# Spreading gate, scale and shift rows over the partitions: by DMA through a DRAM scratch instead of by TensorE

## The reference, cut to what matters

```python
    return rmsnorm(x, final_g)                      # end of the first part
...
    mods = jnp.split(c_silu @ ada_w[layer] + ada_b[layer], N_MOD, axis=-1)
    sh, sc, g = mods[0], mods[1], mods[2]
    h = modulate(rms_norm(x, norm_g[layer, 0]), sh, sc)      # h * (1 + sc) + sh
    x = x + MACARON_WEIGHT * (1.0 + g)[:, None, :] * swiglu(h, ffn_w_in[layer, 0], ffn_w_out[layer, 0])
    ...
    x = x + (1.0 + g)[:, None, :] * y               # y: pool mixer (layer 0) or causal attention (layer 1)
    ...
    x = x + MACARON_WEIGHT * (1.0 + g)[:, None, :] * swiglu(h, ffn_w_in[layer, 1], ffn_w_out[layer, 1])
```

## Time and profile before

| | |
|---|---|
| median of 3 runs | 1232.81 us (1232.74 to 1233.06) |
| the profiled execution | 1232.74 us, of which the span is 1230.9 |
| PE busy | 1199.6 us, 97% of the span |
| DVE, ACT, POOL busy | 66%, 48%, 47% |
| DMA | 293.18 MB, mean 238 GB/s |

### The profile page before, as it was taken

How to read it: one execution, slowest core, us unless ns; L and a number is a source line. 1 busy time by engine, 2 the same in 40 slices (tenths; PEclk the granted TensorE clock), 3 DMA queues, 4 the chain that set the end, 5 groups by cost and what they waited for, 6 DMA issues and landing times.

```text
span 1230.9 us, 15554 instructions
## 1 busy us (share of the span) xinstructions
PE 1199.6 (97%) x5816; PEld 985.0 (80%) x5816; DVE 807.3 (66%) x1116; ACT 592.3 (48%) x774; POOL 577.2 (47%) x424
## 2 busy tenths in 40 slices
PE   9999999999999999899999999999999999999998
PEld 6777887888788887788888878788888887888886
DVE  6885568855687778568778756597774675644433
ACT  5465564555643443454434356444342665534340
POOL 1365333655544534445453455754534463345360
PEclk9999999999999999999999999999999999999999
DMA  9976369744698898439889747699875444766650
GB/s 354 347 255 229 104 235 330 255 172 130 228 339 283 310 330 284 155 95 358 297 296 343 252 171 257 227 315 306 297 291 171 145 135 155 251 209 208 203 171 35
DMA packets 181657, 293.18 MB, mean 238 GB/s; under 512 B 8144, under 2 KB 99920, under 8 KB 181584
## 3 DMA queue, kind: packets, MB, share of 16 engines
q1 hardware_dynamic: 177552, 284.82, 67.7%
q10 hardware_dynamic: 4032, 7.38, 1.8%
HBM read 291.12 MB, written 1.05 MB: 237 GB/s over the span
## 4 chain that ended last, share of the span: by engine, by line
PE 86%; DVE 7%; ACT 3%; issue 2%; POOL 1%; DVEq 0%; ACTq 0%
PE ps L1767 50%; PE ps L1776 25%; PE ps L2027 2%; PE ps L1790 1%; PE ps L1855 1%; DVE w_lo L1129 1%; ACT w_hi L626 1%; PE ps L1912 1%; PE ps L1928 1%; PE ps L1940 1%; POOL w_lo L496 1%; DVE ps L1115 1%; DVE x L1223 1%; PE ps L1951 1%; POOL stat L487 1%
## 5 line engine op out<-in xcount | busy, mean ns | idle before, releaser
L496 POOL TENSOR_TENSOR w_lo<-raw,w_hi 128x512 fp32r<-128x512 f32 x356 | 497.7, 1430 | 448.5 <-ACT w_hi L626 448.5
L1767 PE MATMUL ps<-w_hi,h_hi 128*128 128x512 f32 x1120 | 444.6, 402 | 2.4 <-issue 1.4
L1767 PE MATMUL ps<-w_hi,h_lo 128*128 128x512 f32 x1120 | 432.8, 391 | 0.0
L626 ACT ACTIVATE w_hi<-raw 128x2048 fp32r<-128x2048 f32 x188 | 353.4, 1909 | 87.8 <-PE ps L1776 80.7
L1776 PE MATMUL ps<-w_lo,h_hi 128*128 128x512 f32 x1120 | 301.1, 391 | 5.3 <-DVE w_lo L1129 2.4
L1129 DVE TENSOR_TENSOR w_lo<-raw,w_hi 128x2048 fp32r<-128x2048 f32 x95 | 226.3, 2387 | 97.4 <-ACT w_hi L626 96.7
L1767 PEld LDWEIGHTS ps<-w_hi,h_hi 128*128 128x128 f32 x1120 | 210.3, 188 | 51.6 <-issue 11.2
L1776 PEld LDWEIGHTS ps<-w_lo,h_hi 128*128 128x128 f32 x1120 | 209.5, 188 | 52.4 <-DVE w_lo L1129 3.6
L1767 PEld LDWEIGHTS ps<-w_hi,h_lo 128*128 128x128 f32 x1120 | 211.2, 189 | 40.8
L1115 DVE SCALAR_TENSOR_TENSOR ps<-ada_raw,ccol,ps 128x512 f32<-128x512 f32 x240 | 181.1, 755 | 6.9 <-DMA ada_raw<-ada_w 0.2
L889 ACT ACTIVATE a_hi<-ps 128x512 fp32r<-128x512 f32 x44 | 26.3, 599 | 181.5 <-PE ps L2027 181.5
(11 more groups left out here) (195 smaller groups left out, 1002.6 us busy)
## 6 DMA issues: line engine op xcount, KB each, us to landing
raw<-ffn_in SPq DMA_DIRECT2D x176, 512.0 KB, 5.7
ada_raw<-ada_w SPq DMA_DIRECT2D x144, 512.0 KB, 7.2
raw<-ffn_out SPq DMA_DIRECT2D x44, 1024.0 KB, 5.5
raw<-w_in SPq DMA_DIRECT2D x31, 1024.0 KB, 8.4
raw<-w_out SPq DMA_DIRECT2D x8, 1024.0 KB, 5.9
ada_raw<-kv_ada_w SPq DMA_DIRECT2D x16, 512.0 KB, 7.5
raw<-w_kv SPq DMA_DIRECT2D x8, 1024.0 KB, 5.5
bias<-na_bias ACTq DMA_DIRECT2D x16, 256.0 KB, 3.7
```

The lines of the kernel that those rows point to most:

```text
L496: ins = pool.tensor_tensor(w_lo[:, u % RAW, piece], raw[:, u % RAW, piece], w_hi[:, u % RING, piece].bitcast(F32), ALU.subtract)
L626: act.activation(w_hi[:, u % RING, :], raw[:, u % RAW, :], ACT.Copy).then_inc(*S.inc("w_hi_ready", u))
L1767: pe.matmul(bank(b), part[:, k_in_lhs + k, tok], wh[:, k, c * 512:(c + 1) * 512], start=first_mm[c], stop=False)
```

## The change

The `make_row` function on PE and all its calls go, and `row_copy` on ACT. In their place ACT issues two DMAs per row: `row_store` writes the column block to one row of a scratch tensor `mod_rows` in DRAM, and `row_load`, after a wait for that store, reads this row once for each of the 128 partitions. The final norm's row is loaded from a new kernel input that holds `final_g` as one row. DVE waits for the load's semaphore.

```diff
+        ROWS = {("down", 0, 0): 2, "pool": 5, "pool_scale": 4, "pool_shift": 3, ("down", 0, 1): 8,
+                ("down", 1, 0): 13, "o": 16, ("down", 1, 1): 19}
+        mod_rows = nc.dram_tensor("mod_rows", (len(ROWS), D), F32, kind="Internal").ap()
+        row_of = {name: mod_rows[i:i + 1, :] for i, name in enumerate(ROWS)}
...
-            def row_copy(name, into=row):
-                for half in range(2):
-                    b = job_bank["row", name, half]
-                    act.wait_ge(*S.at("row_done", name, half))
-                    act.activation(into[:, half * 512:half * 512 + 512], bank(b), ACT.Copy).then_inc(
-                        *S.inc("row_ready", name, half))
+            def row_store(name):
+                act.wait_ge(*S.at("mod_ready", ROWS[name]))
+                act.dma_start(row_of[name].rearrange("o (k p) -> p (o k)", p=P), mods[:, ROWS[name], :], allow_slow_non_contiguous=True).then_inc(
+                    row_out[name], 16)
+            def row_load(name, into=row):
+                act.wait_ge(row_out[name], 16)
+                act.dma_start(into[:], row_of[name].broadcast_to([P, D])).then_inc(row_in[name], 16)
...
+                if layer == DEPTH - 1:
+                    act.dma_start(row[:], final_row.broadcast_to([P, D])).then_inc(row_in["final"], 16)
                 o = first["out", layer]
                 fill(o + 3)
...
             fill(first["up", 0, 0])
-            row_copy("final")
...
                 fill(d + 2)
                 high_act(NG - 1)
-                row_copy(("down", layer, i))
+                row_store(("down", layer, i))
+                fill(d + 4)
+                row_load(("down", layer, i))
                 fill(d + NG - 1)
...
-            row_copy("pool", pool_gate)
-            row_copy("pool_scale", pool_rows[:, 0, :])
-            row_copy("pool_shift", pool_rows[:, 1, :])
+            for name, into in (("pool_scale", pool_rows[:, 0, :]), ("pool_shift", pool_rows[:, 1, :]),
+                               ("pool", pool_gate)):
+                row_store(name)
+            for name, into in (("pool_scale", pool_rows[:, 0, :]), ("pool_shift", pool_rows[:, 1, :]),
+                               ("pool", pool_gate)):
+                row_load(name, into)
             norm_stat("pool", 0)
...
             mb_exps(0, 1, (2, 3))
+            row_store("o")
             fill(o + 3)
             mb_exps(1, 0, (0, 1))
             copy_mb_pT(0, 1)
             mb_exps(1, 0, (2, 3))
             copy_q2T(1, 1)
-            row_copy("o")
+            row_load("o")
             copy_mb_pT(1, 0)
...
-                        for half in range(2):
-                            dve.wait_ge(*S.at("row_ready", gate, half))
+                        dve.wait_ge(row_in[gate], 16)
...
-            def make_row(name, col, waits=()):
-                lhs_wait(waits)
-                for half in range(2):
-                    b = job("row", (name, half), ("row_ready", name, half))
-                    for k in range(4):
-                        kk = 4 * half + k
-                        ins = pe.transpose(bank(b)[:, k * P:(k + 1) * P], col[:, kk:kk + 1].broadcast_to([P, P]),
-                                           ident[:])
-                    ins.then_inc(*S.inc("row_done", name, half))
```

More of the change, by code:

```diff
@@ L194, in program @@
             norm_cols, ada_b_cols, c_cols, na_bias, t5_bias, lam_rows, sub_cols, qk_rows,
-            pool_cols, rope, causal, window_weights, identity, out):
+            pool_cols, rope, causal, window_weights, identity, final_row, out):
     units, first = weight_units(w_in, w_out, ffn_in, ffn_out, pool_w, w_kv, w_q, w_o)
@@ L332, in program @@
         x_in_sem = [ctx.enter_context(nc.semaphore(f"x_loaded{t}")) for t in range(NT)]
+        ROWS = {("down", 0, 0): 2, "pool": 5, "pool_scale": 4, "pool_shift": 3, ("down", 0, 1): 8,
+                ("down", 1, 0): 13, "o": 16, ("down", 1, 1): 19}
+        mod_rows = nc.dram_tensor("mod_rows", (len(ROWS), D), F32, kind="Internal").ap()
+        row_of = {name: mod_rows[i:i + 1, :] for i, name in enumerate(ROWS)}
+        row_out = {name: ctx.enter_context(nc.semaphore(f"row_out{i}")) for i, name in enumerate(ROWS)}
+        row_in = {name: ctx.enter_context(nc.semaphore(f"row_in{i}")) for i, name in enumerate((*ROWS, "final"))}
         half_in = ctx.enter_context(nc.semaphore("first_half_loaded"))
@@ L1442, in final_update @@
                 add_final(t)
-                for half in range(2):
-                    dve.wait_ge(*S.at("row_ready", "final", half))
+                dve.wait_ge(row_in["final"], 16)
                 dve.wait_ge(*S.at("x_ready", "fin", t))
@@ L1517, in gate01 @@
                 both = bank(acc_bank[("pool",), t], 2)
-                for half in range(2):
-                    dve.wait_ge(*S.at("row_ready", "pool", half))
+                dve.wait_ge(row_in["pool"], 16)
                 dve.tensor_tensor(both, both, pool_gate, ALU.mult).then_inc(*S.inc("gated01", t))
@@ L1530, in modulate_half @@
                 if t == 0:
-                    dve.wait_ge(*S.at("row_ready", "pool_scale", half))
-                    dve.wait_ge(*S.at("row_ready", "pool_shift", half))
+                    dve.wait_ge(row_in["pool_scale"], 16)
+                    dve.wait_ge(row_in["pool_shift"], 16)
                 link(dve.scalar_tensor_tensor(out=hn[:, t, c], in0=x[:, t, c], scalar=st(t), in1=pool_rows[:, 0, c],
@@ L1999, in _ @@
                     row_pair_half(out_name, 4, i, t, (yn_hi, yn_lo) if half else (h_hi, h_lo), b, 2 * (i % 2))
-                    if s == 3 and layer == DEPTH - 1:
-                        make_row("final", gcols[:, 2, :])
                     if s == 6:
@@ L2041, in after_down @@
                         actT(NG - 1)
[L2042 to L2049, removed]
                 column_product(name, NG, h_ready(norm_name), lambda g: ("act_ready", name, g), after_up)
@@ L2168, in _ @@
             queries_T(1, 1)
-            make_row("o", mods[:, 16, :], [("mod_ready", 16)])
             mb_pT(1, 0)
@@ L2268 @@
         "window_weights": window_weights(),
-        "identity": np.eye(P, dtype=f32),
+        "identity": np.eye(P, dtype=f32), "final_row": get("final_g").reshape(1, D),
     }
```

## The result

The changed kernel takes 1242.49 us (1241.01 to 1247.1, 4 runs) beside 1232.93 for the kernel before; the ratio is 1.0078, 95% interval 1.0062 to 1.0094. It is slower by 9.6 us. The forecast was 1225.0, range 1222 to 1235.

A forecast was written before the change was run, and what follows sets the result against it. PE, busy in 97% of the span, was taken to bound the kernel. Removed slots gain 8.9 us, late pool rows cost 1.1: -7.8 us, from 1232.81 to 1225.0 us, range 1222.0 to 1235.0.

The forecast's parts named there:

- Slots on PE: Removed rows free PE's queue, 0.80 to 0.89 us for most; sum 9.07 us, less 0.2 at "o": 8.9 us.
- The bank wait at "pool_scale": PE's 1.08 us idle inside that row's 2.15 us slot goes with the row; nothing is late in its place.
- The issue on ACT: 17 issues on ACT at 0.33 us, 5.7 us in all, beside PE: 0 except at the pool rows and "o".
- The price of a store, c = 32 ns a packet: Each store is 1024 4-byte packets, 64 per engine, at 32 ns: 2 us plus about 2 of latency.
- The transfers: Prediction step on stores and loads: counted their packets and took c = 32 ns per 4-byte packet into DRAM.
- the sum had 1.1: Pool rows late by 192 c - 5.0, 1.1 us at c = 32 ns, charged because mix(0) has no slack.
- Down products, cost 0: Four down rows: store may take 14 us and lands while ACT copies; cost 0, at worst a few us once.
- The sign given for this part: On ACT, idle time ending with the landing of a store: none in the down stages.
- Rival 2: Between 488 and mix(0): dear 4-byte packets hold up DVE and PE; at 110 ns 16.1 us wait, 1240.0 us; chance 0.18.
- The ends of the range for c (0 to 190 ns): Pool rows: a 4-byte packet's price at its ends; c = 0 costs nothing, 190 ns makes them 31 us late.
- break-even at 72 ns: Pool rows: the packet price c at which their lateness, 192 c - 5.0, uses up the gain of 8.9 us.

The follow-up runs named there:

- e_rowT: Changed kernel with vectors turned by small PE transposes, stored in 512-byte pieces, pool and down (0,0) rows moved to the up product of ffn (0,0): 1224.43 us, ratio 0.9919.
- e_loose: Kernel before plus three 4-byte stores in the up product of ffn (0,0) that nobody waits for until the end: 1240.36 us, ratio 1.0049.
- e_early: Changed kernel with the pool rows' stores and loads some 80 us earlier, in the up product of ffn (0,0): 1234.72 us, ratio 1.0017.
- e_store_early: Changed kernel with only the three pool-row stores moved to the up product of ffn (0,0), their loads left in place: 1231.59 us, ratio 0.9982.

## Why the prediction was wrong

- **Slots on PE (8.9 us).** Right, slot by slot: the table shows 0.8 to 1.0 for each of "final", down (0,0), (0,1), (1,0) and "o", and e_rowT brings 8.7 us of span (1230.9 to 1222.2) with 5 small transposes put back.
- **The bank wait at "pool_scale".** Right: it is gone with the row, and nothing is late in its place in e_rowT.
- **The issue on ACT.** Right: 0.38 us each where the queue is free. In the pool stage three take 3.9 us, over the 1.0 of the sum; the first load had to wait for the first store until 495.0 in any case.
- **The price of a store, c = 32 ns a packet (step "The transfers"): this failed.** Packets take 7 to 9 ns on the engines, under my figure, and yet a store alone takes 8.5 to 10.4 us where 64 x 32 ns + 2 = 4 were expected. The price of a store alone is the crowding of its pieces in DRAM, behind the engines, where I had only a count of packets times a price. And of the other traffic the sum knew only 4 us of full engines that pass first; a single store beside weights took 17.1 us. In the pool stage, with three stores and weights in flight, the 4-byte packets start over 21 us (486.1 to 507.2); most still take 9 ns, but single ones up to 2.9 us. How much of that is the three stores and how much the loads beside them is open. The store that the chain goes through took 20.7 us and the load behind it 9.4; the rows came at 514.9 instead of near 500 (in the kernel before, DVE starts on them 4.5 us behind its product with the gate row, which here starts at 495.6), 14.8 us late where the sum had 1.1.
- **Down products, cost 0.** Right for the change as it was (0.8 to 0.9 gained at each), but by luck of place: three such stores beside a full stream cost 6 us in e_loose, and the store of down (0,1) itself lands in 11.9 us and costs nothing in the changed kernel, but takes 16.8 us in e_early, where ACT comes late from its wait for it and PE loses 3.7 us (4.0 in e_store_early, both between 672 and 695). The sign given for this part, no idle time of ACT behind a store in the down stages, did not come true: ACT waits 22.9 us there in all, and only its slack kept that from PE. That a 4 KB store can pull the stream from some 395 to 98 GB/s was nowhere in my sum; I had added its bytes and packets only.
- **Rival 2** (pool rows late by more than 8.9 us, lower clock behind the wait) is what happened, place and mechanism, at 0.18. The clock cost more than the 1.5 us named there: at least 2.9, up to 3.7. The Trainium skill's warning ("DMA: Bandwidth & Descriptors", Rules for kernel authors: a strided last dimension becomes one descriptor per element; Specifications: under 512 B read-modify-write) pointed the right way. The trace agrees on the count of 1024; the 512 B are not the edge of what was measured here: the 32-byte form lands in 1.4 us, the 4-byte one in 8.5. Whether a read-modify-write is what takes the time, no run shows.
- The ends of the range for c (0 to 190 ns) allowed for a late row of 31 us; the range of the time, cut at 1235, did not. With a price that nothing in the trace bounds, a path without slack and a break-even at 72 ns, 0.18 was too little.

## What to carry to other kernels

Look at how densely the small pieces of a store lie in DRAM: here a transposing store in packed 4-byte pieces was slow to land by itself and slowed the loads beside it, awaited or not. Turn the vector first (one small transpose), store in long pieces, let the DMA do the copying to all partitions, and issue it when the data is ready rather than ahead of the use. Where an operation's price is not in the trace and its path has no slack, the chance of the bad case is not small.

## What the runs showed of the hardware that I had not expected

- Writes of 4 bytes to DRAM: 8.5 us for 16 in 64 bytes, 4.3 for 8, 3.1 for 4, 2.5 for 2, though the engines are done after 0.7 us. For 16 in 64 bytes it is 7.6 to 8.5 us whatever their number between 256 and 1024.
- While such stores are under way beside a full weight stream, the loads slow down: 98 GB/s where the kernel before has 401 (420 to 424 us, e_loose).
- A DVE product of 128 x 1024 with one operand in SBUF read in steps of 32 bytes takes 2.16 us instead of 1.23.
- PE's granted clock stood at 0.50 in 516 to 522, behind an idle time of 14.2 us, and at 0.50 in 311 to 314 behind 2.2 us.
